# Moving the gate projection of six of eight heads from the in-projection into the recurrence of a gated DeltaNet layer

## What is computed

```python
proj = xn @ w_in                          # q, k, v, z: 8 heads x 128 columns each, then b and a
qkv, new_buf = causal_conv(proj[..., :3 * GDN_DIM], conv_buf, conv_w)
q, k, v = jnp.split(jax.nn.silu(qkv), 3, axis=-1)
q = l2norm(q) * (GDN_DK ** -0.5);  k = l2norm(k)
beta = sigmoid(b);  g = -exp(a_log) * softplus(a + dt_bias)
o, S = gated_delta_chunked(q, k, v, beta, g, S0, chunk)
o = rmsnorm(o, g_out) * silu(z)           # z is the gate; it is wanted here for the first time
y = o.reshape(B, T, GDN_DIM) @ w_out
```

## Time and profile before

| | us |
|---|---|
| median of three runs | 3988.22 (3984.44 to 3998.23) |
| the profiled execution, its span | 3986.4 |
| in-projection of the 32 channels on PE | 53.3 to 299.3 |
| recurrence | 301.9 to 645 |
| all that follows | 645 to 3986.4 |

### The profile page before, as it was taken

How to read it: one execution, slowest core, us unless ns; L and a number is a source line. 1 busy time by engine, 2 the same in 40 slices (tenths; PEclk the granted TensorE clock), 3 DMA queues, 4 the chain that set the end, 5 groups by cost and what they waited for, 6 DMA issues and landing times. The chain is left out here.

```text
span 3986.4 us, 45941 instructions
## 1 busy us (share of the span) xinstructions
PE 3005.8 (75%) x14557; PEld 1439.4 (36%) x14557; DVE 2474.6 (62%) x6084; ACT 1535.0 (39%) x4402; POOL 1289.7 (32%) x1172
## 2 busy tenths in 40 slices
PE   7997888777666677768757798776777876666666
PEld 6886775322212122223313575322232222222221
DVE  2665443676676667767773343476677677667675
ACT  2352121444343344446432221344544444334332
POOL 0004330444434333333441110233334344334433
PEclk9998788988778788888878898888888988787778
DMA  2211002999999999999996453799999999999998
GB/s 89 73 51 55 13 13 71 404 420 416 420 414 418 405 397 387 411 366 384 402 421 244 165 204 144 291 375 390 381 375 415 405 404 421 413 420 413 411 421 334
DMA packets 234350, 1261.33 MB, mean 316 GB/s; under 512 B 32008, under 2 KB 71952, under 8 KB 97552
## 3 DMA queue, kind: packets, MB, share of 16 engines
q0 software_dynamic: 153600, 1133.58, 69.8%
q1 hardware_dynamic: 80528, 125.08, 9.1%
HBM read 1244.25 MB, written 14.19 MB: 316 GB/s over the span
## 5 line engine op out<-in xcount | busy, mean ns | idle before, releaser
L1951 PE MATMUL acc<-ring,diag 128*64 128x512 f32 x4096 | 1339.0, 751 | 751.3 <-ACT diag L1650 748.9
L1569 POOL DMA_INDIRECT ring<-in_uv,idx x1024 | 1119.1, 1093 | 1895.3 <-PE acc L1951 1635.2
L1761 DVE SCALAR_TENSOR_TENSOR ring<-ring,rep 128x1024 f32<-128x1024 f32 x1024 | 1230.6, 1221 | 368.9 <-DMA ring<-in_uv,idx 309.3
L1951 PEld LDWEIGHTS acc<-ring,diag 128*64 128x64 f32 x4096 | 250.3, 158 | 1494.2 <-ACT diag L1650 1317.8
L1642 ACT ACTIVATE hg<-hs 128x1 f32<-128x1 f32 x1024 | 203.7, 199 | 1141.1 <-DVE ring L1761 1139.1
L1650 ACT ACTIVATE diag<-const,hgg 128x64 f32<-128x64 f32 x1024 | 356.4, 348 | 33.4
L1646 ACT ACTIVATE hgg<-hg,weigh_by 128x1 f32<-128x1 f32 x1024 | 302.0, 295 | 33.2
L1883 PE MATMUL big<-xnT,w 128*128 128x264 f32 (+1 forms) x960 | 297.1, 435 | 0.0
L1883 PEld LDWEIGHTS big<-xnT,w 128*128 128x128 f32 x960 | 174.8, 203 | 185.0 <-issue 166.4
L298 PE MATMUL acc<-xnT,w 128*128 128x260 f32 x1024 | 230.2, 386 | 0.7 <-ACT inp L419 0.7
L298 PEld LDWEIGHTS acc<-xnT,w 128*128 128x128 f32 x1024 | 196.3, 192 | 38.4 <-issue 7.5
(11 more groups left out here) (571 smaller groups left out, 4057.7 us busy)
## 6 DMA issues: line engine op xcount, KB each, us to landing
w<-in_w_peer SPq DMA_DIRECT2D x64, 512.0 KB
w<-in_w_gdn SPq DMA_DIRECT2D x32, 512.0 KB, 3.6
ring<-in_uv,idx POOLq DMA_INDIRECT x1024, 12.3
wo<-in_w_mla_out SPq DMA_DIRECT2D x8, 1024.0 KB, 11.5
wo<-in_w_uq SPq DMA_DIRECT2D x8, 768.0 KB, 14.2
out_ssm_s<-states SPq DMA_DIRECT2D x4, 1024.0 KB, 5.1
wo<-in_w_gdn_out SPq DMA_DIRECT2D x4, 1024.0 KB, 8.2
sk<-in_keys SPq DMA_DIRECT2D x64, 64.0 KB
```

The lines of the kernel that those rows point to most:

```text
L1569: pool.indirect_dma_start(out=ring[:, c % RING, :], out_offset=None, in_=uv, in_offset=bass.IndirectOffsetOnAxis(ap=idx[u % 2][:, c:c + 1] ...
L1761: dve.scalar_tensor_tensor(ring[:, c % RING, 0:D], ring[:, c % RING, 0:D], 1.0, rep[:, 2 * a + c // RING, :], ALU.mult, ALU.mult, accum_ou ...
L1951: last = pe.matmul(acc[i][rows(j), :], diag[:, r, :], ring[:, r, D + HALF * j:D + HALF * j + HALF], start=r == 0, stop=r == RING - 1)
```

## The change

- `gdn_in` does 26 channels instead of 32: the gate of heads 0 and 1 stays. The sixteen norms go to channels 8 to 23, one each, and the small chain of the decays to channels 12 to 20. The convolution of the sample rows (L374, L377) comes ahead of the last norm. SP's loop over the weights is written out.
- `gdn_seq` makes the gate of the next pair in pairs 0, 1 and 2: head a = 1 in level 0 (into pD, one half of the rows ahead of each head's transposes), head a = 0 behind the transposes of the output (into pC). ACT applies Silu to each. Two weight buffers `wz` of 4 KB per partition are filled by SP.
- Sample states are held in two buffers of a pair each. Pairs 0 and 1 are asked for at the start, pair i + 1 once pair i - 1 has been read and stored.
- `on` takes the place of `qdT` and `u` that of `eG`; `xnT` (and `wz`) live through the recurrence.

```diff
-NORMS = {10: 0, 11: 1, 13: 2, 14: 3, 16: 4, 17: 5, 19: 6, 20: 7, 22: 8, 23: 9, 24: 10, 25: 11, 26: 12, 27: 13, 28: 14, 29: 15}
+NORMS = {8 + j: j for j in range(2 * H)}
+EARLY_Z = 2
-    NC, PAD = KINDS * H, CW - 1
+    NC, PAD = QKV + EARLY_Z, CW - 1
...
@@ gdn_seq, ScalarE
+                def z_out(i, a, banks):
+                    n = 3 * H + 2 * i + 2 + a
+                    z = chan(n)
+                    after(act, (s["z_made"], 2 * i + 2 - a))
+                    act.activation(z[:, 0:PART], banked(banks, 0), ACT.Silu)
+                    act.activation(z[:, PART:], banked(banks, 1)[:, 0:SEQ - PART], ACT.Silu)
+                    act.activation(Fs[:, n, :], banked(banks, 1)[:, SEQ - PART:], ACT.Silu).then_inc(s["z_out"], 1)
...
+                        if j == 0 and i < PAIRS - 1:
+                            z_out(i, 1, pD)                 # behind joined_out of level 0
...
+                    if i < PAIRS - 1:
+                        z_out(i, 0, pC)                     # behind o_root, the last of the pair
...
@@ gdn_seq, TensorE
+                def gate_rows(a, banks, r):
+                    for kk in range(KD):
+                        last = pe.matmul(banked(banks, r), wz[:, a, kk, :], xnT[:, kk, PART * r:PART * r + PART], start=kk == 0, stop=kk == KD - 1)
+                    return last
...
+                    after(pe, (s["z_out"], 2 * i))          # ahead of the products of keys into pC
...
                         for a in range(2):
+                            if j == 0 and i < PAIRS - 1:
+                                after(pe, at("products", i, 2 * a + 2), at("wz1", i, 16))
+                                last = gate_rows(1, pD, a)
+                                if a:
+                                    last.then_inc(s["z_made"], 1)
                             after(pe, at("seeded", i, 2 * a + 2) if j == 0 else at("grown", i, 2 * (j - 1) + a + 1))
                             turn(pC[a], U[a]).then_inc(s["flipped"], 1)
...
+                            if j == 1 and i < PAIRS - 1:
+                                after(pe, (s["z_out"], 2 * i + 1))
                             change(i, j - 1)
...
                         turn(pA[a], on[a]).then_inc(s["o_turned"], 1)
+                    if i < PAIRS - 1:
+                        after(pe, at("wz0", i, 16))
+                        gate_rows(0, pC, 0)
+                        gate_rows(0, pC, 1).then_inc(s["z_made"], 1)
...
@@ gdn_seq, SyncE
+                old(0)                                      # old: one pair's states; gate: one head's weights
+                gate(0, 1)
+                gate(0, 0)
+                old(1)
                 for i in range(PAIRS):
+                    if i and i < PAIRS - 1:
+                        after(sp, at("d_o", i, 0), at("kept", i, 0))
+                        old(i + 1)
+                    if i < PAIRS - 2:
+                        after(sp, (s["z_made"], 2 * i + 1))
+                        gate(i + 1, 1)
                     for a in range(2):
                         after(sp, at("state", i, 2 * (NT - 1) + a + 1))
                         sp.dma_start(core.o["ssm_p"][2 * i + a], S[a][:, NT, :]).then_inc(s["stored"], 16)
+                    if i < PAIRS - 2:
+                        after(sp, (s["z_made"], 2 * i + 2))
+                        gate(i + 1, 0)
                     after(sp, at("d_new", i, GP))
```

More of the change, by code:

```diff
@@ L281, in _ @@
                 sp.dma_start(gout[:, :], core.i["g_out"]).then_inc(s["gate_in"], 16)
[L282 to L285, removed]
+                for n in range(W, NC):
+                    sp.wait_ge(made, n - W + 1)
+                    sp.dma_start(w[:, n % W, :, :], core.i["w_gdn"][n]).then_inc(landed[n % W], 16)
                 sp.wait_ge(kept, QKV)
@@ L372, in _ @@
                         normal(j)
[L373 to L382, removed]
+                    if n == 12:
                         dve.wait_ge(s["gate_in"], 48)
@@ L411, in _ @@
                         then(dve.tensor_copy(cols[:, 4:6, :], ex[:, 1:3, :]))
+                dve.wait_ge(sraw, QKV)
+                dve.tensor_tensor(prod[:, :, :, :], taps[:, :, :, :],
+                                  cw[:, :].rearrange("p (c j o) -> p c j o", j=CW, o=1).to_broadcast([P, QKV, CW, NS]), ALU.mult).then_inc(sconv, 1)
+                dve.wait_ge(sconv, 1)
+                dve.tensor_reduce(Fs[:, 0:QKV, :], prod[:, :, :, :].rearrange("p c j b -> p c b j"), AX.X, ALU.add).then_inc(sconv, 1)
+                for j in here(QKV - 1):
+                    normal(j)
             @block.scalar
@@ L458, in _ @@
                         act.activation(alog[:, :], alog[:, :], ACT.Exp).then_inc(s["acts"], 1)
+                    if n == 13:
+                        act.wait_ge(s["step"], 3)
+                        act.activation(neg[:, :, :], neg[:, :, :], ACT.Exp).then_inc(s["acts"], 1)
+                    if n == 15:
+                        act.wait_ge(s["step"], 4)
+                        act.activation(neg[:, :, :], neg[:, :, :], ACT.Ln).then_inc(s["acts"], 1)
+                    if n == 19:
+                        act.wait_ge(s["step"], 15)
+                        act.activation(ex[:, :, :], ex[:, :, :], ACT.Exp).then_inc(s["acts"], 1)
+                        act.activation(srep[:, 1, :], psum[:, 2, H * NS:], ACT.Exp).then_inc(s["acts"], 1)
+                smooth(QKV - 1, (QKV - 1) % 2, chan(QKV - 1))
+                roots(QKV - 1)
+                for n in range(QKV, NC):
                     after(act, (made, n + 1))
@@ L463, in _, with gdn_seq @@
                     act.activation(Fs[:, n, :], acc[n % 2][:, 1, SEQ - PART:], ACT.Copy).then_inc(raw, 1)
[L464 to L474, removed]
                 act.wait_ge(raw, NC)
                 act.wait_ge(sconv, 2)
-                act.activation(Fs[:, :, :], Fs[:, :, :], ACT.Silu).then_inc(silu, 1)
-def gdn_seq(core, oT, F, Fs, cols, srep, gout, os):
+                act.activation(Fs[:, 0:NC, :], Fs[:, 0:NC, :], ACT.Silu).then_inc(silu, 1)
+def gdn_seq(core, xnT, wz, oT, F, Fs, cols, srep, gout, os):
     nc = core.nc
@@ L550, in group, with held, banked @@
             return slice(n, n + G)
+        def held(i, m=0, count=G):
+            n = HELD * (i % 2) + G * m
+            return states[:, n:n + count, :]
+        def banked(banks, r):
+            return banks[r][:, :, :].rearrange("p t c -> p (t c)")[:, 0:PART]
         def wide(tile):
@@ L569, in _ @@
                     for m in range(GP):
-                        mine = states[:, group(i, m), :]
+                        mine = held(i, m)
                         pool.tensor_tensor(mine, mine, wide(srep[:, 1, group(i, m)]), ALU.mult).then_inc(s["faded"], 1)
@@ L639, in change @@
                         out = made_in[m][:, j, :]
-                        pe.matmul(out, nkb[:, n:n + 1].to_broadcast([P, P]), states[:, n, :], start=True, stop=False)
+                        pe.matmul(out, nkb[:, n:n + 1].to_broadcast([P, P]), held(i, m)[:, j, :], start=True, stop=False)
                         last = pe.matmul(out, bv[:, n:n + 1].to_broadcast([P, P]), core.ident, start=False, stop=True)
@@ L648, in read @@
                         n = GP * G * i + j
-                        last = pe.matmul(pD[0][:, 0, j:j + 1], states[:, n, :], q[:, n:n + 1], start=True, stop=True)
+                        last = pe.matmul(pD[0][:, 0, j:j + 1], held(i, 0, HELD)[:, j, :], q[:, n:n + 1], start=True, stop=True)
                     last.then_inc(s["d_o"], 1)
+                def gate_rows(a, banks, r):
+                    for kk in range(KD):
+                        last = pe.matmul(banked(banks, r), wz[:, a, kk, :], xnT[:, kk, PART * r:PART * r + PART], start=kk == 0, stop=kk == KD - 1)
+                    return last
                 pe.wait_ge(s["d_square"], 1)
```

40 lines of the change are left out of this document (24 added, 16 removed).

## The result

| | before | after |
|---|---|---|
| median of four runs each | 3993.22 us (3984.44 to 4007.5) | 3945.33 us (3940.61 to 3949.62) |
| ratio, 95% interval | | 0.9881 [0.9863, 0.9898] |
| span of the profiled execution | 3986.4 | 3938.5 |

The kernel became 47.9 us faster by the medians and by the profiled spans; the sum of the prediction was 48.8. A second comparison in five rounds gave 0.9879 [0.9855, 0.9903]. So the total came as forecast, but not all of its terms did. The difference of 1.2% is clear of the scatter: the interval leaves out 1.

The account below looks back on a forecast made before the run. PE was taken to bound the in-projection, with idle and half-clock PE stretches in the recurrence. Terms -46.0 + 7.4 - 10.2 = -48.8 us took the 3986.4 span to 3937.6, median 3939; range 3927 to 3960.

Parts of the forecast that it names:

- Six channels and the wait at channel 25: In-projection: six channels fewer save 42.1 us, the vanished wait for ACT's squares 4.3, less 0.4; 46.0 shorter in sum.
- steps 2 and 3: In-projection: no wait for ACT's squares at channel 25 gives 4.3 us; a norm beside channels 8 to 23 costs about 0.4.
- ACT's lateness at channel 13: In-projection: ACT's extra tables and tiny activations, placed at channel 12, make PE wait about 0.4 us once.
- DVE's lag: In-projection: DVE's round is 0.7 us longer than PE's, but the lag does not add up; cost 0, otherwise 11 us.
- rival B: In-projection: DVE becomes the bound, its round 8.58 us against 7.87; only 38 us saved, 3950; chance 0.08.
- The end of a pair: Gate passes behind the output's transposes delay the chain by 1.6, 2.9 and 2.9 us; cost 7.4.
- Level 0: Gate passes filling PE's wait for head 0's U keep the clock up; 3.4 us saved per pair, 10.2 in three.
- a clock of 0.5 in the gate's passes: Recurrence: listed among the signs that would show the forecast wrong.
- R as a whole: The recurrence, before 343.1 us: 7.4 us lost at pair ends, 10.2 saved in level 0; near 340 us expected.
- ACT's Silu in level 0: Between level 0's last copy and level 1's first: table load and activations end near 331.8, just hidden; with drain, 1.4 us late.
- Transfers: Gate weights and sample states arrive in time; cost 0, a late one would show as POOL waiting.
- The total: Whole kernel: 48.8 us shorter, a span of 3937.6 and a median of 3939.

Follow-up runs that it names:

- norms_only: Changed kernel with all 32 channels in the in-projection and no gate in the recurrence; new norm order and two state buffers kept: span 3995.8 us, recurrence 345.9.
- end_one: Changed kernel with all but one slice of eight of the gate passes behind the output's transposes left out: span 3937.8 us, recurrence 327.8.

## Why the prediction was right, and where its steps were off

- **Six channels and the wait at channel 25** (-46.0): measured -44.5. The 7.01 us a channel held, and the wait for ACT's squares went. Missed was the wait of 1.0 us ahead of L321 at channel 17: the step costed the decay chain on ACT, and not what DVE's four small steps at channel 16, behind its norm, do to PE. norms_only parts the two: the six channels are 246.9 - 204.1 = 42.8 us (42.1 predicted), and the new order alone gives 1.7 to 1.8 us, where steps 2 and 3 summed to 3.9. ACT's lateness at channel 13 cost 0.5 (0.4 predicted). DVE's lag did not hold PE back, with 7.87 us a round to the last norm: rival B is out.
- **The end of a pair** (+7.4): L683 came 3.5 us later (3.4 predicted) and at full speed. Leaving the passes out gained 6.0 to 9.7 us in pairs 0 to 2, which holds the 7.4: the mechanism and the size were right, as far as one trace of end_one tells.
- **Level 0** (-10.2): in pair 0 DVE's last read of pD ends at 278.32 + 0.68 = 279.00 (the row stands below), so it is 10.6 us to `change`, and before it was 337.63 - 323.48 = 14.1: 3.5, and 3.4 was predicted. In pairs 1 and 2 of the first trace the clock fell in the first half of the passes, which lost 1.7 and 1.5 us, as the text held possible and the sum left out; a clock of 0.5 in the gate's passes stood among its signs of being wrong, and there it was so for some 3.5 us. That leaving them out costs 20 to 30 us was not foreseen, nor that they are worth 12 to 18 with no passes at the end: the prediction took the clock's fall at a place as it was before, and priced the two kinds of passes apart.
  Timeline of DVE in level 0 of pair 0 after, head a = 1 (answers to the earlier trace rows):

```profile
278.32 0.68 DVE L795 TENSOR_TENSOR qk<-pD,dec 128x512 f32<-128x512 f32 x1
```

- **R as a whole** (-2.8): measured +2.8 and +2.9, and -3.8 in one trace. In the first trace pairs 0 to 2 together give -2.6, near the sum. What failed was that pair 3 and the last read, which have no gate passes, would stay as they were. They took 2.9 and 2.5 us more: the clock was down for longer in pair 3 (23.5 and 13.9 us against 17.0 and 10.4), and the last read ran at 0.50. norms_only shows the same excess without any gate pass.
- **ACT's Silu in level 0**: predicted just hidden. It ended at 287.29 + 0.18 = 287.5, and T's copy started at 287.35; the transposes that this copy reads had started at 286.6 and take 0.6, so it is late by 0.2 us at most. The table load takes 1.28 us and the next activation starts 0.02 behind it. The 1.38 us of drain of the Trainium skill (ScalarE: Activation LUTs, What ACT_TABLE_LOAD costs) is not seen here; going by the row was right.
- **Transfers**: no engine waited for a transfer within R in the traces.
- **The total**: -44.5 + 2.8 - 6.2 = -47.9. That it met 48.8 to 1 us is luck in good part, since B's scatter made up for what R and A had missed; without B it is -41.7. That it lay near there is not luck: it rests on the 7.01 us a channel, and over three traces A and R together gave -41.7, -48.7 and -41.4 against the first trace of the kernel before.

## What to carry to other kernels

An idle stretch of TensorE ahead of a dense chain cost twice here: the wait itself, and a clock of 0.5 in what came behind it, for 17 us and more. Work moved into such a stretch can be worth more than its own time: here it is 3 x 7 us of passes, and with seven eighths of them left out the stage is 20 to 30 us longer. The same passes put where the wait is shorter than they are cost 6 to 10 us in three pairs. When pricing a change, price the clock in the stretches that the change does not touch too, and don't add up the prices of two changes to the clock as if they were apart. Take two or three traces before a few microseconds are called a gain.

## What the runs showed of the hardware that was not expected

- The clock fell with PE never idle: behind 32 passes of one column (3.7 us) it went to 0.50. With the same passes 128 columns wide, which took the same 3.6 us, it stayed at 1.00. R was 9 to 19 us shorter by that edit alone, in one trace.
- Matmuls whose result nobody reads can pay: with 7 us of them in level 0 of pair 3 the stretch from the second transposes to `change` took 6.9 us instead of 12.6, and the pair was not longer but 2 to 5.6 us shorter.
- One and the same program had a stage of 343 us twice and of 336 once, while another had its 340.1 twice, and once more with a later start, within 0.1 us.
